# The eight output units of the second block in plain fp32 instead of split products

## The reference

```python
def token_mixers(z, k1, k2, v, rope, lam, lam_init, ..., w_out):
    a_val, a_gate, q, _, _, u, sv, bg, cg, xin = z
    y_a = conformer_conv(a_val, a_gate, conv_a_w, conv_a_b, ln_a_g, ln_a_b)
    q1, q2 = qk_heads(q, rope)
    y_b = diff_attention(q1, q2, k1, k2, v, lam, lam_init, subln_g)
    y_c = spatial_gating(u, sv, sg_ln_g, sg_ln_b, sg_w, sg_b)
    y_d = short_conv_mixer(bg, cg, xin, conv_d_w)
    return jnp.concatenate([y_a, y_b, y_c, y_d], axis=-1) @ w_out

def channel_mixer(h, w1, w2):
    return jnp.square(jax.nn.relu(h @ w1)) @ w2

...
        x = x + mod_x[2] * token_mixers(zx, k1, k2, v, *mix_args)
        x = x + mod_x[5] * channel_mixer(modulate(rms_norm(x, norm2_g[l]), mod_x[3], mod_x[4]),
                                         mlp_w1[l], mlp_w2[l])
```

## Time and profile before

| what | us |
|---|---|
| median of 3 runs | 1747.14 |
| lowest, highest | 1745.61, 1747.72 |
| span of the profiled execution | 1743.0 |
| TensorE busy in it | 1645.8 (94%) |
| VectorE busy | 879.1 (50%) |
| ScalarE busy | 547.1 (31%) |

### The profile page before, as it was taken

The page is one execution under the profiler, slowest core; times in us unless marked ns, Lnnn a source line. Parts: engine busy times, 40 slices in busy tenths (PEclk is TensorE's granted clock), DMA queues, the critical chain, the costliest instruction groups (busy, mean ns, idle before and its releaser), DMA issues.

```text
span 1743.0 us, 30482 instructions
## 1 busy us (share of the span) xinstructions
PE 1645.8 (94%) x13036; PEld 1254.3 (72%) x13036; DVE 879.1 (50%) x1720; ACT 547.1 (31%) x947; POOL 59.2 (3%) x112
## 2 busy tenths in 40 slices
PE   6999999999999889988999999999999999999998
PEld 3789767565555555555555556968999998599998
DVE  4414554324552212211121125997888787787776
ACT  3224422311310200000000003556555554574443
POOL 0000000100000000000000000000000000000000
PEclk9999999899999999999999999999999999999999
DMA  9953667999999999999999999554454452745430
GB/s 389 362 231 121 263 269 330 366 424 425 424 424 425 423 425 425 424 425 425 424 425 424 425 425 393 219 205 163 168 194 179 158 193 84 304 171 186 176 145 24
DMA packets 65589, 526.58 MB, mean 302 GB/s; under 512 B 6458, under 2 KB 15930, under 8 KB 28352
## 3 DMA queue, kind: packets, MB, share of 16 engines
q1 hardware_dynamic: 51312, 471.18, 66.7%
q0 software_dynamic: 14160, 53.70, 7.6%
HBM read 523.81 MB, written 1.05 MB: 301 GB/s over the span
## 4 chain that ended last, share of the span: by engine, by line
PE 65%; DMA 25%; DVE 7%; ACT 2%; issue 1%; SPq 0%; DVEq 0%; ACTq 0%
PE bank L903 65%; DMA big<-in_w_exp_down 9%; DMA big<-in_w_exp_up 6%; DMA big<-in_w_exp_gate 6%; DMA big<-in_w_ada 1%; DVE big L2942 1%; DVE w_lo L2331 1%; DMA big<-in_ada_half 1%; DMA big<-in_ada_w 1%; DVE big L2331 1%; DVE big L2999 1%; ACT w_hi L2150 0%; DVE big L3074 0%; DVE big L3058 0%; DVE big L2813 0%
## 5 line engine op out<-in xcount | busy, mean ns | idle before, releaser
L903 PE MATMUL bank<-big 128*32 128x352 f32 (+11 forms) x7432 | 957.5, 415 | 80.3 <-DMA big<-in_w_exp_down 25.7
L903 PEld LDWEIGHTS bank<-big 128*32 128x32 f32 (+6 forms) x7432 | 574.0, 142 | 442.3 <-issue 278.8
L2331 DVE TENSOR_TENSOR w_lo<-big,w_hi 128x1024 fp32r<-128x1024 f32 x212 | 257.5, 1221 | 121.5 <-ACT w_hi L2291 53.1
L903 PE MATMUL bank<-h_lo,w_hi 128*128 128x256 f32 (+1 forms) x1040 | 296.6, 285 | 0.0
L903 PE MATMUL bank<-h_hi,w_hi 128*128 128x256 f32 (+1 forms) x896 | 256.8, 287 | 6.4 <-DVE h_lo L2331 2.8
L903 PE MATMUL bank<-h_hi,w_lo 128*128 128x256 f32 (+1 forms) x896 | 254.5, 284 | 0.0
L903 PEld LDWEIGHTS bank<-h_lo,w_hi 128*128 128x128 f32 x1040 | 199.0, 191 | 0.7
L2331 DVE TENSOR_TENSOR big<-big 128x256 f32<-128x256 f32 (+6 forms) x219 | 112.8, 522 | 152.4 <-ACT big L2126 130.1
L903 PEld LDWEIGHTS bank<-h_hi,w_hi 128*128 128x128 f32 x896 | 170.8, 191 | 10.3 <-DVE h_lo L2331 4.8
L2291 ACT ACTIVATE w_hi<-big 128x1024 fp32r<-128x1024 f32 x120 | 127.0, 1058 | 146.8 <-PE bank L903 146.8
L903 PEld LDWEIGHTS bank<-h_hi,w_lo 128*128 128x128 f32 x896 | 171.1, 191 | 0.7
(11 more groups left out here) (266 smaller groups left out, 1373.3 us busy)
## 6 DMA issues: line engine op xcount, KB each, us to landing
big<-in_w_exp_gate SPq DMA_DIRECT2D x64, 1408.0 KB, 21.9
big<-in_w_exp_up SPq DMA_DIRECT2D x64, 1408.0 KB, 21.4
big<-in_w_exp_down SPq DMA_DIRECT2D x48, 1536.0 KB, 22.2
big<-in_mlp_w SPq DMA_DIRECT2D x32, 2048.0 KB, 7.8
big<-in_w_in SPq DMA_DIRECT2D x17, 2048.0 KB, 8.4
big<-in_u_w POOLq DMA_DIRECT2D x64, 512.0 KB, 9.2
big<-in_w_ada SPq DMA_DIRECT2D x12, 2048.0 KB, 12.5
big<-in_ada_w SPq DMA_DIRECT2D x12, 2048.0 KB, 9.5
```

The costliest lines, as they stand in the source:

```text
L903: return nc.tensor.matmul(o, l, r, start=start, stop=stop)
L2331: return V.tensor_tensor(o, a, b, op)
```

## The change

The eight output units of both layers are multiplied as plain fp32 matmuls, one call per step in place of three, from the loaded weights and from `mix` itself. `h_high`, `h_low`, `w_high` and `w_low` of these units go. The numbering of splits closes up (the MLP's units follow unit 19), so ScalarE makes the high parts of MLP units 0 to 3 in one go behind its SiLU, and VectorE their low parts in the first four turns of the residual's loop. The output's two slots are freed when TensorE has finished units 23 and 27, and SyncE issues the load of the first down block (slot 2) behind the other down block.

```diff
@@ SyncE
                     load(q % 3, slot(q % 3, KT, 512),
                          ap["w_in_2"][layer, q] if q < 5 else ap["w_out_2"][layer, q - 5],
-                         units_split(layer, 4 * (q + 1)))
+                         units_split(layer, 4 * (q + 1)) if q < 5 else (S("tile_in"), OUT2_AT[layer] + 4 * (q - 4)))
...
                 halves(h0 + 3, (12, 24)[layer])
-                mlp_load(0, 2)
                 sp.wait_ge(S("mix2_ready"), layer + 1)
                 sp.wait_ge(S("ya_ready"), layer + 1)
                 mlp_load(0, 3)
+                mlp_load(0, 2)
                 mlp_load(0, 1)
@@ TensorE
-                ts = units_begin(20, 4, "D")
+                def out_product(j, t, x):
+
+                    k = MIX_ORDER[x]
+                    m = mm(PB[t % 4][:, 0:nf], proj_unit(layer, j)[:, k, :], mix[:, k, 0:nf], x == 0, x == KT - 1)
+                    if x == KT - 1:
+                        m.then_inc(S("tile_in"), 1)
...
-                units_product(20, ts, MIX_ORDER[0], hb, True, False)
+                ts = out_begin()
+                pe.wait_ge(S("yd_ready"), layer + 1)
+                out_products(ts, 0, 1)
                 weigh_values(len(units) - 2)
-                units_product(20, ts, MIX_ORDER[1], hb + 1, False, False)
+                out_products(ts, 1, 2)
...
+                pe.wait_ge(S("yc_ready"), layer + 1)
+                out_products(ts, 2, 4)
+                ada_cols(ADA2_LAST[layer])
+                keep_busy(2, 5)
+                pe.wait_ge(S("ya_ready"), layer + 1)
+                out_products(ts, 4, 6)
+                pe.wait_ge(S("mix2_ready"), layer + 1)
+                for n, t in enumerate(ts):
+                    for x in (6, 7):
+                        out_product(20 + n, t, x)
+                for n in range(4):
+                    if n == 0:
+                        s, loads = part_place(layer, 6)
+                        pe.wait_ge(S(f"slot_full{s}"), 16 * (loads + 1))
+                    t = tiles.add("D")
+                    bank_free(t)
+                    for x in range(KT):
+                        out_product(24 + n, t, x)
@@ ScalarE
-                        if j < 18:
+                        if j < 16:
                             w_high(layer, j + NWB)
...
-                w_high(layer, 18 + NWB)
...
-                    if u == 0:
-                        w_high(layer, 19 + NWB)
...
-                    if u == 5:
-                        act.wait_ge(S("yd_ready"), layer + 1)
-                        h_high(MIX_ORDER[:2])
...
+                for q in range(NWB):
+                    w_high(layer, 20 + q)
                 for q in range(KT):
-                    w_high(layer, 20 + q + NWB)
@@ VectorE
                     if x == 0:
                         link(i_)
-                        w_low(layer, 16 + NWB)
                 i_.then_inc(S("qk2_ready"), 1)
-                w_low(layer, 17 + NWB)
...
                     if u == 3:
-                        w_low(layer, 18 + NWB)
...
                     if u == 5:
-                        w_low(layer, 19 + NWB)
...
-                    if u == 6:
-                        h_low(0)
-                        h_low(1)
...
-                    w_low(layer, 20 + dt + NWB)
+                    if dt < NWB:
+                        w_low(layer, 20 + dt)
```

More of the change, by code:

```diff
@@ L530, in build, with part_place @@
         mlp_loads = []
+        def part_place(layer, q):
+            s = q % 3
+            return s, mlp_loads[layer][s] - (7 - s + 2) // 3 + q // 3
         def linker(eng, name):
@@ L1742, in _, with out_begin, out_products @@
                         weigh_values(u - 2)
-                ts = units_begin(20, 4, "D")
+                def out_begin():
+                    ts = [tiles.add("D") for _ in range(4)]
+                    for t in ts:
+                        bank_free(t)
+                    s, loads = part_place(layer, 5)
+                    pe.wait_ge(S(f"slot_full{s}"), 16 * (loads + 1))
+                    return ts
+                def out_product(j, t, x):
[3 more added lines that the diff above has]
+                        m.then_inc(S("tile_in"), 1)
+                def out_products(ts, first, last):
+                    for x in range(first, last):
+                        for n, t in enumerate(ts):
+                            out_product(20 + n, t, x)
                 pe.wait_ge(S("exp_done"), u0 + len(units))
-                hb = KT + 24 * layer + KT
-                units_product(20, ts, MIX_ORDER[0], hb, True, False)
+                ts = out_begin()
+                pe.wait_ge(S("yd_ready"), layer + 1)
+                out_products(ts, 0, 1)
                 weigh_values(len(units) - 2)
-                units_product(20, ts, MIX_ORDER[1], hb + 1, False, False)
+                out_products(ts, 1, 2)
                 for n in ADA2_TAIL[layer]:
@@ L2143, in w_high @@
                 if j % 4 == 0:
-                    s = j // 4 % 3 if j < 28 else MLP_SEM[0]
-                    loads = mlp_loads[layer][s] - (7 - s + 2) // 3 + j // 12 if j < 28 else mlp_loads[layer][s]
+                    s, loads = part_place(layer, j // 4) if j < 20 else (MLP_SEM[0], mlp_loads[layer][MLP_SEM[0]])
                     act.wait_ge(S(f"slot_full{s}"), 16 * (loads + 1))
@@ L2897, in w_low @@
                 dve.wait_ge(S("w_hi_ready"), split_no(layer, j + 1))
-                tt(proj_split(w_lo, j), proj_unit(layer, j) if j < 28 else w_unit(j - 28),
+                tt(proj_split(w_lo, j), proj_unit(layer, j) if j < 20 else w_unit(j - 20),
                    proj_split(w_hi, j).bitcast(F32), ALU.subtract).then_inc(S("w_lo_ready"), 1)
```

50 lines of the change are left out of this document (13 added, 37 removed).

## The result

| what | before | after |
|---|---|---|
| median of 17 runs each, us | 1745.83 | 1751.14 |
| lowest, highest | 1743.85, 1751.74 | 1746.65, 1753.66 |
| ratio after / before | | 1.0022, 95% interval 1.0015 to 1.003 |
| span of the profiled execution | 1743.0 | 1745.8 |
| VectorE, ScalarE busy | 879.1, 547.1 | 856.3, 527.1 |

The changed kernel is 0.22% slower, 3.8 us by the ratio, and the interval (2.6 to 5.2 us) leaves out zero. The medians lie 5.3 us apart, the means 3.8: the times of a kernel spread over 7 to 8 us. VectorE does 22.8 us less and ScalarE 20 us less, and the kernel is longer all the same.

A forecast was written before the change was run, and what follows sets the result against it. Bound by TensorE from output units 24 to 27 on, VectorE in layer 0's attention, a modulation-weight DMA in layer 1's. 2.2 + 2.2 - 1.4 = +3.0 us: span 1746.0, with the 4.1 offset 1750.1 us; range 1746.5 to 1754.0.

The forecast's parts named there:

- The products, +2.2 a layer: Output products in each layer: plain steps add 4.0 us of matmul time, vanished idle pieces take off 1.8.
- No wait is left: TensorE's output products: mixed rows arrive in time, so no idle remains; row 0 can cost 0.5 us at most.
- products over 31 us: Sign in the profile after, from first output product to MLP, that would speak for rival 2.
- VectorE in layer 0, -1.4: Layer 0's attention: removed subtractions gain 0.66 us before the scores and 0.8 in unit 3; bounds 0 to 2.4.
- Rival 2: VectorE gives nothing back in layer 0, or products cost the full 4.6 us; +4.4 to +5.6, 1752 us, chance 0.16.
- VectorE in layer 1, 0: Layer 1's attention: removed subtractions gain 0, as VectorE waited for TensorE, which hung on a 10.88 us DMA.
- The loads, 0: SyncE's later down and up weight loads, for slots 2 and 0, still arrive in time for the MLP: 0 us.
- Rival 1: The late load stalls the MLP, 2.2 us in layer 1 and nothing in layer 0; 1752.3 us, chance 0.12.
- Rival 3: Freed VectorE time counts in full in both layers, 4.7 us a layer; -5.0, 1742.1 us, chance 0.07.
- 4: Rival: weight loads don't hide behind plain passes, 128 steps; +49 us, near 1799 us, chance 0.01.
- Rival 5: Plain products run at one pass, 0.12 us a step; 31 us less, 1719 us, chance 0.01.
- Layer 1's attention unmoved: Expected in the profile after: layer 1's attention keeps its length; a shorter one would speak for rival 3.

The follow-up runs named there:

- filled kernels: Kernel before and changed kernel, each with extra filler matmuls at three places where TensorE stood idle; 1746.28 us (0.9996) and 1750.33 us (1.0022).
- late block: Layer 1's first 2 MB MLP load issued behind all the attention's modulation loads; changed kernel 1746.37 us (1.0000), kernel before 1744.69 us (0.9989).

## Why the prediction was right, and where it was so by luck

The forecast was 1750.1 us (1746.5 to 1754.0), the measurement 1751.14, and +3.0 against +3.8 (2.6 to 5.2). That the two times lie only 1 us apart is luck: the forecast starts from the median of three runs, 1747.14, and the median of seventeen is 1745.83; from there +3.0 makes 1748.8. The 4.1 us that it took as an offset between span and time are none: in each execution of which both are known the two are 1.8 to 1.9 us apart, and the profiled one was merely a short one. Its likeliest class was "within 0.2%", with 0.42 on slower; the ratio lies at that line, on the slower side of it. By its steps:

- **The products, +2.2 a layer.** Measured 2.23 and 2.25. That is no luck, since it came from rebuilding the whole stretch, 30.7 us against 28.45, and the 30.7 was right. What was wrong is its division, by 0.6 each way. The matmul term was put at 4.0, which is only 2.2 + 1.8; by the prediction's own step prices it is 64 x (0.430 - 0.359) = 4.5, and its lower bound 64 x (0.427 - 0.359) = 4.4 and not 3.8. Measured it is 4.6. The waits were put at -1.8, the idle pieces of the earlier trace rows; they are -2.4 by the run that left out the splits and kept the form. The rows held that already: 64 x 0.359 and the 3.16 us between the products make 26.1, and of 28.45 that leaves 2.3 for waits. The missing 0.6 is what idle pieces don't count: the start behind each wait, and 0.28 behind the head norm's sum.
- **"No wait is left".** Right: TensorE is one piece of 225.10 us, and that was so even with products 4.6 us faster, so rows 0 to 3 were there sooner than I had reckoned: without splits TensorE takes row 0 at 1191.71, 13.75 us after the restart, where I had it ready 15.6 after. The sign "products over 31 us" would have been a wrong one: layer 1 was forecast at 31.8 and is there at 31.9 by the same count.
- **VectorE in layer 0, -1.4.** The trace has 0.66 ahead of the scores (modulation step to scores 1.66, then 1.00 us) and 0.54 in unit 3, where I had 0.8; put back, 1.04 in all. (The prediction adds 0.66 and 0.8 up to 1.4, and they make 1.46.) Rival 2 falls, which gave nothing here; its other half, products at the full 4.6, came true, and the larger waits paid for it. Of unit 3 the step that failed is the end of the layer norm's sum: VectorE still waited 0.51 for it.
- **VectorE in layer 1, 0.** Right, with its reason: load 18 binds. With the load moved away, the four subtractions are worth 0.3.
- **The loads, 0.** The up block for slot 0 was issued as the MLP began, at 1550.8 to 1551.1. ScalarE waited 1.06 us for it, TensorE not at all. Rival 1 falls. Rival 3 falls with the subtractions put back, 4 and 5 with the +2.2 of the products. (Rival 5's time takes 31 us off the forecast; off the kernel before they make 1716.)
- **"Layer 1's attention unmoved".** By the first pair of profiles this was wrong by 1.2 us, and I would have put it on the change if the kernel before had not been profiled again. Its second profile has the same low clock behind load 18, and the same length of C.

So the change is +4.6 of matmul form twice, -2.4 of waits for splits twice, -1.1 of VectorE in layer 0: +3.3, and +3.8 (2.6 to 5.2) was measured.

What the prediction missed is above it. It took the wait for load 18 as what makes VectorE's relief worthless in layer 1, and went on. Moving one load on SyncE was worth 3.8 us in the changed kernel, as much as the whole change, and 1.9 in the kernel before.

## What to carry to other kernels

Taking work off VectorE and ScalarE pays only as far as TensorE waited for it: here 22.8 us of VectorE time were worth 1.1 us of attention and 2 x 2.4 of waits, and the dearer matmul form that bought it cost 2 x 4.6. Use the dearer form on those operands alone that are waited for (8 steps of 64 in each layer took 1.9 us off in all), and price the two halves of such a trade with one run each: the cheap form with the preparation left out, and the preparation put back. Count such a stretch from start to start, since idle pieces alone gave 1.8 of 2.4 us here. Before a difference of one or two microseconds between two profiles is given to a change, take a second profile of the kernel before; and look first at the wait that you use as a cover.

## What the runs showed of the hardware

- A plain fp32 step of 128x128x256 costs 0.072 us more than the three rounded matmuls of a split one (4.61 us over 64 steps), nothing of it hidden.
- In these profiles the granted clock fell to half for some 3.4 us behind TensorE gaps of 1.0 to 2.6 us, and the instructions behind took 0.8 to 1.6 us longer each time. In layer 0's attention, behind a gap of 1.8 us, it lasted some 7 us in three profiles, and 48 instructions took 3.2 us longer. It isn't fixed to a gap: the same kernel had it at 1486 in one profile and at 1500 in the next, and the gap of 1.8 us that ends at 1157 to 1162 was followed by a fall in the second profile of the kernel before, in both filled kernels and with the late block, and by none in the first profiles of before and after. The filled gaps had no fall behind them.
- A transfer of 1 MB behind one of 2 MB on the queue took 11 to 14 us from its issue. With the 2 MB moved behind them, the nine of that stretch took 5 to 9.
